# Three layers on one core: the frequency-domain convolution run one half of its frequencies at a time, and an output projection whose first tiles are split in two

## Chip, cores, metric

The kernel runs on one core of one Trainium2 chip. The metric is device time in microseconds (us) of one execution; lower is better.

## What is computed

The reference is a stack of three layers on 512 tokens of 1024 channels, float32. The change lies in the mixer of the first layer, which is two mixers side by side (512 channels each), joined by an output projection:

```python
def _hyena(hy, spec, skip):
    L = hy.shape[1]
    u = hy.astype(jnp.float32)
    z, g1, g2 = u[..., :D_HYENA], u[..., D_HYENA:2 * D_HYENA], u[..., 2 * D_HYENA:]
    for o, gate in enumerate((g1, g2)):
        conv = jnp.fft.irfft(jnp.fft.rfft(z, n=2 * L, axis=1) * spec[:, o], n=2 * L, axis=1)[:, :L]
        z = gate * (conv + z * skip[o].astype(jnp.float32))
    return z

...
        y_hy = _group_rms_norm(_hyena(hy, spec, hy_skip[l]), hy_norm_g[l], HYENA_GROUPS)
...
        y_ml = _group_rms_norm(y_ml, ml_norm_g[l], MLSTM_HEADS)
        mixed = jnp.concatenate([y_hy.astype(h.dtype), y_ml.astype(h.dtype)], axis=-1)
        h = h + mixed @ w_out[l]
```

`spec` is the spectrum of a filter that a small network with sine activations makes from the position, times a decay window. `_group_rms_norm` divides groups of channels by their root mean square. `y_ml` is a gated linear attention; after this layer's mixer come a cross-attention over 256 memory rows, a feed-forward layer, and then a second block of two layers, none of which the change touches.

## The kernel before

Every engine has a program of its own, written out in order; semaphores tie them together. A projection's weights come as panels of 1 MB that SyncE loads into two buffers in turn (`load`, L2556: panel g waits until panel g-2 has been split). ScalarE makes the upper half-precision part of a panel and VectorE the lower one (`split`, L1155 and L1706); TensorE then takes three half-precision products for each pair of tiles (`product`, L366). TensorE writes into two rings of banks of its accumulator memory: ring A with four banks, ring B with three. `reuse` waits until the bank's reader of one turn before has freed it.

The stage that the change touches runs from 259.3 us (the last gate projection `og` ends) to 448.7 us (the sum for the norm of the memory rows begins). Its steps on TensorE, in order, are these:

1. `filters(0)` (L659): eight products make the taps of order 0, four tiles (`tt`) by two directions. VectorE multiplies each with its window and adds and subtracts pairs (`filter_windows`, L2067; `taps`, L2060) into `HS` and `HD`.
2. `head_sums("ml")` (L639) sums the squares of the attention's output, `turn_z(0)` (L670) transposes `z`. ScalarE takes the root (L1200), VectorE its reciprocal (`inverse_rows`, L1798), and `head_roots("ml")` (L647) spreads the result over the partitions. VectorE scales with it (L2098) and makes the lower parts (`low`, L1724); these are input tiles 4 to 7 of the output projection.
3. For each of two orders `o`: `transform("spec")`, the spectrum of the taps, then `transform("zspec")`, the spectrum of z (both L694). Each is cosine and sine (`part`) by even and odd positions (`odd`) by two halves of the frequencies (`kt`), thus eight banks of two products. ScalarE copies each even bank to `EVEN` (L1195); VectorE adds and subtracts the odd bank (`butterfly`, L2117 and L2118), which gives a frequency and its mirror image. Then VectorE takes the complex product: `multiply` (L2126 to L2136), 12 instructions for a half, and `mirror` (L2142, L2143), 4 instructions for a half, which raises the semaphore `mirrored`.
4. The transform back (L711): TensorE waits for `mirrored` of a half and takes that half for all four channel tiles. VectorE adds the skip (L2169), GpSimd multiplies with the gate (L2492), which gives the z of the next order. Between the orders come `filters(1)` and `turn_z(1)`.
5. `head_sums("hy")`, root, reciprocal and `head_roots("hy")` for the convolution's output, input tiles 0 to 3 of the projection (`hy_low`).
6. `project("out", 8, ...)`: tiles 0 and 1 of panel 0 together, over all eight input tiles, then tiles 2 and 3 of panel 1, one after the other. Then `middle` takes the sum for the memory norm (`norm_sum`, L500), which waits for squares that ScalarE makes after it has split three panels (L1434 to L1440), and the last two panels follow in halves of the tokens.

TensorE's and VectorE's loops over one order, as before:

```python
                transform("spec", (HS, HD))
                pe.wait_ge(B.freed_sem(("zt", o, 3)), B.freed_at(("zt", o, 3)))
                transform("zspec", (ZT, ZT))
...
                for kt in range(2):
                    if kt + o:
                        dve.wait_ge(sem("sine_parts"), 4 * o + 2 * kt)
                    for part in range(2):
                        butterfly("zspec", kt, part, ZSP[:, 2 * part, :], ZSP[:, 2 * part + 1, :])
                    when_free(dve, A, ("zspec", o, kt, 1, 1))
                    multiply(2 * kt)
                    if kt:
                        mirror(0)
                    multiply(2 * kt + 1)
                mirror(1)
```

## Time and profile before

| | |
|---|---|
| median of 3 runs | 2122.17 us (2120.74 to 2129.97) |
| the profiled execution | 2120.89 us, span 2119.0 us |
| mean granted clock of TensorE | 0.981 |
| TensorE busy, whole span | 2028.9 us (96%) |
| the stage 259.3 to 448.7 | 189.4 us, TensorE busy 153.09 us |

PE is TensorE, DVE is VectorE, ACT is ScalarE, POOL is GpSimd, SP is SyncE. In the timelines one float32 product of the program is two instructions. A row's time in brackets is how long the engine had stood idle, and the arrow names what released it. In the view by stretches the granted clock is a share of full speed: 1.00 is 2.4 GHz, 0.50 is 1.2 GHz.

### The profile page before, as it was taken

The numbers are of one execution on the slowest core, as the hardware profiler recorded it, in microseconds if no ns is written. First come the engines' busy times: TensorE is split into PE (matmuls) and PEld (weight loads), VectorE is DVE, ScalarE is ACT, GpSimd is POOL, SyncE is SP. The second block draws the span as 40 slices with busy tenths as digits, with TensorE's granted clock in tenths as the row PEclk, the third lists the DMA queues.
The fourth block names the chain that finished last, engine by engine and source line by source line (L and its number), as shares of the span: only waits on it lengthen the run. The fifth ranks groups of instructions, "written<-read, shape, count | busy, mean of one in ns | idle before, by whom it ended". The sixth has DMA issues, their size and how long they took to land.

```text
span 2119.0 us, 27115 instructions
## 1 busy us (share of the span) xinstructions
PE 2028.9 (96%) x11486; PEld 1199.2 (57%) x11486; DVE 946.1 (45%) x1209; ACT 726.8 (34%) x1121; POOL 351.1 (17%) x358
## 2 busy tenths in 40 slices
PE   7999988699999999999999999999999899999997
PEld 5644435366667444488456644446866566444466
DVE  5654565645545333225475422222655645222224
ACT  5432220134434442114363422221454534222213
POOL 1011200011003221003102512110240016121100
PEclk9999988899999999999999999999999999999999
DMA  6211210022222222232222232222221121233321
GB/s 233 80 60 40 77 42 0 0 100 100 100 102 78 100 100 100 100 103 103 75 80 80 76 104 100 100 100 100 80 80 60 40 80 60 99 103 106 111 100 41
DMA packets 28179, 179.65 MB, mean 85 GB/s; under 512 B 2912, under 2 KB 7136, under 8 KB 7136
## 3 DMA queue, kind: packets, MB, share of 16 engines
q1 hardware_dynamic: 27264, 170.93, 23.4%
q10 hardware_dynamic: 512, 4.94, 0.7%
q0 software_dynamic: 288, 2.10, 0.3%
q8 instruction: 91, 1.49, 0.3%
q14 instruction: 24, 0.20, 0.0%
HBM read 175.86 MB, written 2.10 MB: 84 GB/s over the span
## 4 chain that ended last, share of the span: by engine, by line
PE 87%; DVE 9%; ACT 3%; issue 1%; DMA 0%; POOL 0%; ACTq 0%; DVEq 0%
PE psum_a L368 24%; PE psum_a L369 24%; PE psum_a L370 24%; PE psum_b L500 2%; PE psum_a L694 2%; PE psum_a L711 2%; DVE X L1730 1%; PE psum_a L622 1%; PE psum_den L620 1%; DVE RINV L1704 1%; PE psum_a L647 1%; DVE W_PARTS L1710 1%; PE psum_b L600 1%; DVE ARENA L1730 1%; ACT W_PARTS L1160 1%
## 5 line engine op out<-in xcount | busy, mean ns | idle before, releaser
L1710 DVE SCALAR_TENSOR_TENSOR W_PARTS<-W,W_PARTS 128x2048 f16<-128x2048 f32 x145 | 332.6, 2297 | 614.6 <-ACT W_PARTS L1160 614.6
L368 PE MATMUL psum_a<-U,W_PARTS 128*128 128x512 f16 (+1 forms) x1304 | 489.6, 375 | 8.8 <-POOL U L2464 3.9
L369 PE MATMUL psum_a<-U,W_PARTS 128*128 128x512 f16 (+1 forms) x1304 | 489.4, 375 | 0.0
L370 PE MATMUL psum_a<-U,W_PARTS 128*128 128x512 f16 (+1 forms) x1304 | 489.1, 375 | 0.0
L1160 ACT ACTIVATE W_PARTS<-W 128x2048 f16<-128x2048 f32 x145 | 275.7, 1905 | 502.1 <-PE psum_a L370 502.1
L368 PE MATMUL psum_a<-ARENA,W_PARTS 128*128 128x256 f16 (+2 forms) x956 | 295.4, 309 | 3.6 <-DVE W_PARTS L1710 3.0
L369 PE MATMUL psum_a<-ARENA,W_PARTS 128*128 128x256 f16 (+2 forms) x956 | 295.3, 309 | 0.0
L370 PE MATMUL psum_a<-ARENA,W_PARTS 128*128 128x256 f16 (+2 forms) x956 | 295.3, 309 | 0.0
L368 PEld LDWEIGHTS psum_a<-U,W_PARTS 128*128 128x128 f16 x1304 | 128.1, 98 | 158.9 <-DVE W_PARTS L1710 9.6
L370 PEld LDWEIGHTS psum_a<-U,W_PARTS 128*128 128x128 f16 x1304 | 128.1, 98 | 148.2 <-issue 1.6
L369 PEld LDWEIGHTS psum_a<-U,W_PARTS 128*128 128x128 f16 x1304 | 128.1, 98 | 147.4 <-issue 3.8
L2498 POOL TENSOR_TENSOR ARENA<-ARENA 128x512 f16<-128x512 f32 x76 | 118.1, 1574 | 450.4 <-ACT ARENA L1256 450.4
L368 PEld LDWEIGHTS psum_a<-ARENA,W_PARTS 128*128 128x128 f16 (+1 forms) x956 | 93.8, 98 | 49.7 <-DVE W_PARTS L1710 3.3
L368 PE MATMUL psum_a<-MIX,W_PARTS 128*128 128x256 f16 (+1 forms) x384 | 118.8, 309 | 2.1 <-DVE MIX L1724 1.5
L370 PEld LDWEIGHTS psum_a<-ARENA,W_PARTS 128*128 128x128 f16 (+1 forms) x956 | 93.9, 98 | 45.1 <-issue 0.6
L369 PEld LDWEIGHTS psum_a<-ARENA,W_PARTS 128*128 128x128 f16 (+1 forms) x956 | 93.9, 98 | 44.7 <-issue 0.3
L370 PE MATMUL psum_a<-MIX,W_PARTS 128*128 128x256 f16 (+1 forms) x384 | 118.8, 309 | 0.0
L369 PE MATMUL psum_a<-MIX,W_PARTS 128*128 128x256 f16 (+1 forms) x384 | 118.8, 309 | 0.0
L1247 ACT ACTIVATE ARENA<-psum_a 128x512 f32<-128x512 f32 (+1 forms) x84 | 45.7, 552 | 191.8 <-PE psum_a L370 191.7
L2460 POOL TENSOR_TENSOR U<-X,U 128x256 f16<-128x256 f32 x64 | 48.5, 772 | 215.8 <-ACT U L1170 170.5
L1195 ACT ACTIVATE ARENA<-psum_a 128x256 f32<-128x256 f32 (+2 forms) x79 | 35.5, 467 | 128.2 <-PE psum_a L370 83.8
L1889 DVE SCALAR_TENSOR_TENSOR ARENA<-psum_a,ARENA 128x512 f32<-128x512 f32 (+1 forms) x48 | 30.8, 646 | 101.1 <-PE psum_a L370 101.1
(289 smaller groups left out, 2709.2 us busy)
## 6 DMA issues: line engine op xcount, KB each, us to landing
W<-weights SPq DMA_DIRECT2D x159, 1024.0 KB, 4.8
CON<-const ACTq DMA_DIRECT2D x1, 3071.5 KB, 12.2
X<-x_in SPq DMA_DIRECT2D x2, 1024.0 KB, 7.3
U<-dft POOLq DMA_DIRECT2D x1, 1024.0 KB, 5.3
ARENA<-dft POOLq DMA_DIRECT2D x1, 1024.0 KB, 5.2
ARENA<-mem_in ACTq DMA_DIRECT2D x1, 1024.0 KB, 4.7
y_out<-U SPq DMA_DIRECT2D x2, 512.0 KB, 3.0
y_out<-U SPq DMA_DIRECT2D x4, 256.0 KB, 2.2
```

Source lines behind the costliest of these rows:

```text
L368: nc.tensor.matmul(out, left(0), right(0), start=first, stop=False)
L369: nc.tensor.matmul(out, left(0), right(1), start=False, stop=False)
L370: return nc.tensor.matmul(out, left(1), right(0), start=False, stop=last)
L500: last = nc.tensor.matmul(bank[:, 0:HALF], ones, square_tile(kt), start=kt == 0, stop=kt == KT - 1)
L694: last = nc.tensor.matmul(bank[:, :], FDFT[:, part, odd, n, kt * P:(kt + 1) * P], sources[part][:, 2 * odd + n, :], start=n == 0, stop=n == 1)
L711: last = nc.tensor.matmul(banks[ct][:, HALVES[odd]], y[:, 2 * odd + kt, ct * P:(ct + 1) * P], IDFT[:, part, kt, HALVES[odd]], start=kt + p ...
L1160: nc.scalar.activation(HOMES[home_of[g]][:, 0, :], W[g % 2][:, :], ACT.Copy, scale=W_SCALE).then_inc(sem("panel_high"), 1)
L1247: nc.scalar.activation(TS[:, 2 * (j % 2) + m, cols], A.bank(key)[:, 0:cols.stop - cols.start], ACT.Silu if M.gated else ACT.Relu, scale=DE ...
L1710: nc.vector.scalar_tensor_tensor(out=home[:, 1, :], in0=W[g % 2][:, :], scalar=W_SCALE, in1=home[:, 0, :], op0=ALU.mult, op1=ALU.subtract) ...
L1730: nc.vector.scalar_tensor_tensor(out=out(kt, half), in0=src(kt, half), scalar=par(gain, kt), in1=RINV[:, HALVES[half]], op0=ALU.mult, op1= ...
L2460: nc.gpsimd.tensor_tensor(out, src(kt, half), high_part, ALU.subtract).then_inc(sem(f"low_{name}"), 1)
L2498: nc.gpsimd.tensor_tensor(G16[:, 1, n, :], GF[:, n % 4, :], G16[:, 0, n, :], ALU.subtract)\
```

## The change

The same products, copies and element-wise instructions are issued. Their order, some of their buffers and two rings change:

- Each order runs by halves of the frequencies: spectrum of z half 0, of the taps half 0, of z half 1, of the taps half 1. VectorE multiplies and mirrors half 0 before it comes to the taps' half 1. The product tiles of half 0 have buffers of their own (`SQ`, `ROOT`, `RINV`), as `HS` and `HD` are still being read.
- `turn_z(0)` moves ahead of `filters(0)`. `head_roots("ml")` moves behind the first half of z's spectrum; on VectorE the reciprocal, the scaling and the lower parts move with it.
- Three of the eight tap products of order 1 run between the two halves of the transform back of order 0, on ring B. The split of panel 1 of the output projection (`used(("og", 1))`) moves on VectorE from ahead of order 0 to the end of order 0.
- The first four tiles of the output projection each take input tiles 4 to 7 first (`out_tile`): tile 0 ahead of `head_sums("hy")`, tiles 1 and 2 behind it, tile 3 behind `head_roots("hy")`, which now writes to ring B; then each takes input tiles 0 to 3.

```diff
-        YC, YS = HS, HD
+        early = SQ[:, :, :].rearrange("p a b -> p (a b)").rearrange("p (a b) -> p a b", a=2)
+        YC = (early[:, 0, :], HS[:, 1, :], early[:, 1, :], HS[:, 3, :])
+        YS = (ROOT[:, :], HD[:, 1, :], RINV[:, :], HD[:, 3, :])
...
+        def filter_ring(o, tt, d):
+            return B if o and 2 * tt + d < 3 else A
...
-            def filters(o):
-                for tt in range(4):
-                    for d in range(2):
-                        bank = reuse(A, ("filt", o, tt, d))
-                        c = SMALL_W3 + (2 * o + d) * 512
-                        nc.tensor.matmul(bank[:, :], HID[0:64, token_tile(tt)], SMALL[0:64, c:c + 512], start=True, stop=True)\
-                            .then_inc(A.done, 1)
+            def filters(o, numbers):
+                for n in numbers:
+                    tt, d = divmod(n, 2)
+                    R = filter_ring(o, tt, d)
+                    bank = reuse(R, ("filt", o, tt, d))
+                    c = SMALL_W3 + (2 * o + d) * 512
+                    nc.tensor.matmul(bank[:, :], HID[0:64, token_tile(tt)], SMALL[0:64, c:c + 512], start=True, stop=True)\
+                        .then_inc(R.done, 1)
...
+            turn_z(0)
             pe.wait_ge(sem("sine"), 2)
-            filters(0)
+            filters(0, range(8))
             head_sums("ml", 4, lambda h: EVEN[:, h, :], one_row)
-            turn_z(0)
-            head_roots("ml", 4, ROWS[0:64, 3, :], row_back)
+            pe.wait_ge(sem("fdft_landed"), 16)
             for o in range(2):
-                if o:
-                    filters(1)
-                    turn_z(1)
+                pe.wait_ge(B.freed_sem(("zt", o, 3)), B.freed_at(("zt", o, 3)))
+                transform("zspec", o, 0, (ZT, ZT))
                 if o == 0:
-                    pe.wait_ge(sem("fdft_landed"), 16)
+                    head_roots("ml", 4, ROWS[0:64, 3, :], row_back)
                 pe.wait_ge(sem("taps"), 8 * (o + 1))
-                def transform(what, sources):
-                    for kt in range(2):
-                        for part in range(2):
-                            for odd in range(2):
-                                bank = reuse(A, (what, o, kt, part, odd))
-                                for n in range(2):
-                                    last = nc.tensor.matmul(bank[:, :], FDFT[:, part, odd, n, kt * P:(kt + 1) * P],
-                                                            sources[part][:, 2 * odd + n, :], start=n == 0, stop=n == 1)
-                                last.then_inc(A.done, 1)
-                transform("spec", (HS, HD))
-                pe.wait_ge(B.freed_sem(("zt", o, 3)), B.freed_at(("zt", o, 3)))
-                transform("zspec", (ZT, ZT))
+                transform("spec", o, 0, (HS, HD))
+                transform("zspec", o, 1, (ZT, ZT))
+                transform("spec", o, 1, (HS, HD))
                 if o == 0:
                     pe.wait_ge(sem("idft_landed"), 16)
-                banks = [reuse(A, ("y", o, ct)) for ct in range(4)]
-                for kt in range(2):
-                    pe.wait_ge(sem("mirrored"), 2 * o + kt + 1)
-                    for ct in range(4):
-                        for odd in range(2):
-                            for part, y in ((0, HC), (1, HSN)):
-                                last = nc.tensor.matmul(banks[ct][:, HALVES[odd]], y[:, 2 * odd + kt, ct * P:(ct + 1) * P],
-                                                        IDFT[:, part, kt, HALVES[odd]], start=kt + part + odd == 0, stop=kt + part + odd == 3)
-                        if kt == 1:
-                            last.then_inc(A.done, 1)
+                inverse_transform(o, 0)
+                if o == 0:
+                    filters(1, range(3))
+                inverse_transform(o, 1)
+                if o == 0:
+                    filters(1, range(3, 8))
+                    turn_z(1)
...
+            def out_tile(j, tiles):
+                if len(out_panels) <= j // 2:
+                    w, g = panel()
+                    panel_of.setdefault("out", g)
+                    out_panels.append((w.rearrange("p l (k c) -> p l k c", k=KT), g))
+                w, g = out_panels[j // 2]
+                bank = A.bank(("out", j)) if ("out", j) in A.at else reuse(A, ("out", j))
+                for kt in tiles:
+                    pe.wait_ge(sem("hy_low" if kt < 4 else "ml_low"), kt % 4 + 1)
+                    last = product(bank[:, :], lambda l: w[:, l, kt, (j % 2) * P:(j % 2 + 1) * P], lambda l: MIX16[:, l, kt, :],
+                                   kt == 4, kt == 3)
+                    if kt == 3:
+                        last.then_inc(A.done, 1)
+                        released[g] = A.done, A.at["out", j] + 1
+            out_tile(0, range(4, 8))
             head_sums("hy", 4, lambda h: PR[h], lambda ct: half[:, 62 - 2 * ct:126 - 2 * ct])
-            head_roots("hy", 4, ZT[0:64, 0, :], lambda ct: gback[:, ct, :])
-            project("out", 8, MIX16, first_wait=lambda kt: pe.wait_ge(sem("hy_low" if kt < 4 else "ml_low"), kt % 4 + 1),
-                    tail="x", middle=lambda: norm_sum("mem", 0))
+            out_tile(1, range(4, 8))
+            out_tile(2, range(4, 8))
+            head_roots("hy", 4, ZT[0:64, 0, :], lambda ct: gback[:, ct, :], B)
+            out_tile(3, range(4, 8))
+            for j in range(4):
+                out_tile(j, range(4))
+            tile_list["out"] = [(("out", j), j, slice(0, T), j // 2 if j % 2 else None) for j in range(4)]
+            project("out", 8, MIX16, tail="x", middle=lambda: norm_sum("mem", 0), first=2)
...
+            def turned(o):
+                for tt in range(4):
+                    copy_out(B, ("zt", o, tt), ZT[:, tt, :], B.bank(("zt", o, tt))[:, :])
+            def even_copies(what, o, kt):
+                for part in range(2):
+                    if what == "spec":
+                        when_free(act, A, ("zspec", o, kt, part, 1))
+                    elif o:
+                        when_free(act, A, ("spec", 0, kt, part, 1))
+                    key = (what, o, kt, part, 0)
+                    copy_out(A, key, EVEN[:, 2 * kt + part, :], A.bank(key)[:, :])
+            turned(0)
...
-            used(("og", 1))
-            for tt in range(4):
-                copy_out(B, ("zt", 0, tt), ZT[:, tt, :], B.bank(("zt", 0, tt))[:, :])
-            for h in range(4):
-                key = ("rn", "ml", h)
-                high(A.freed_sem(key), A.freed_at(key), MIX16[:, 0, 4 + h, :], QK[:, h, :], "ml_high")
             for o in range(2):
-                for tt in range(4 * o):
-                    copy_out(B, ("zt", o, tt), ZT[:, tt, :], B.bank(("zt", o, tt))[:, :])
-                for what in ("spec", "zspec"):
-                    for kt in range(2):
-                        for part in range(2):
-                            n = 2 * kt + part
-                            if what == "zspec":
-                                when_free(act, A, ("spec", o, kt, part, 1))
-                            elif o:
-                                when_free(act, A, ("zspec", 0, kt, part, 1))
-                            key = (what, o, kt, part, 0)
-                            copy_out(A, key, EVEN[:, n, :], A.bank(key)[:, :])
+                even_copies("zspec", o, 0)
+                if o == 0:
+                    for h in range(4):
+                        key = ("rn", "ml", h)
+                        high(A.freed_sem(key), A.freed_at(key), MIX16[:, 0, 4 + h, :], QK[:, h, :], "ml_high")
+                even_copies("spec", o, 0)
+                even_copies("zspec", o, 1)
+                even_copies("spec", o, 1)
+                if o == 0:
+                    used(("og", 1))
+                    turned(1)
             for ct in range(4):
                 act.wait_ge(sem("z_gated"), 5 + ct)
...
-                high(A.freed_sem(key), A.freed_at(key), MIX16[:, 0, ct, :], HY[:, ct, :], "hy_high")
+                high(B.freed_sem(key), B.freed_at(key), MIX16[:, 0, ct, :], HY[:, ct, :], "hy_high")
...
-            filter_windows(0)
-            inverse_rows("ml", ROWS[0:64, 3, :], ROWS[0:64, 2, :])
...
-                low("ml_high", h + 1, MIX16[:, 1, 4 + h, :], QK[:, h, :], MIX16[:, 0, 4 + h, :], "ml_low")
-            used(("og", 1))
-            for o in range(2):
-                if o:
-                    filter_windows(1)
...
-                def multiply(n):
-                    kt, sign = n // 2, n % 2
+            def multiply(o, kt):
+                when_free(dve, A, ("spec", o, kt, 1, 1))
...
...
+            dve.wait_ge(sem("ml_gated"), 4)
+            for o in range(2):
+                butterflies("zspec", o, 0)
+                if o == 0:
+                    inverse_rows("ml", ROWS[0:64, 3, :], ROWS[0:64, 2, :])
+                    ml_norm()
+                    dve.wait_ge(sem("ml_low"), 4)
                 dve.wait_ge(sem("taps"), 8 * (o + 1))
+                butterflies("spec", o, 0)
+                multiply(o, 0)
+                dve.wait_ge(sem("sine_parts"), 4 * o + 2)
+                butterflies("zspec", o, 1)
+                mirror(o, 0)
+                butterflies("spec", o, 1)
+                multiply(o, 1)
+                mirror(o, 1)
                 if o == 0:
-                    dve.wait_ge(sem("ml_low"), 4)
-                for kt in range(2):
-                    for part, h in ((0, HC), (1, HSN)):
-                        butterfly("spec", kt, part, h[:, kt, :], h[:, 2 + kt, :])
-                for kt in range(2):
-                    if kt + o:
-                        dve.wait_ge(sem("sine_parts"), 4 * o + 2 * kt)
-                    for part in range(2):
-                        butterfly("zspec", kt, part, ZSP[:, 2 * part, :], ZSP[:, 2 * part + 1, :])
-                    when_free(dve, A, ("zspec", o, kt, 1, 1))
-                    multiply(2 * kt)
-                    if kt:
-                        mirror(0)
-                    multiply(2 * kt + 1)
-                mirror(1)
+                    filter_windows(1, range(3))
...
+                if o == 0:
+                    dve.wait_ge(sem("mirrored"), 2)
+                    filter_windows(1, range(3, 8))
+                    used(("og", 1))
             inverse_rows("hy", ZT[0:64, 0, :], ZT[0:64, 1, :])
             for ct in range(4):
-                scale_rows(("rn", "hy", ct), HY[:, ct, :], HY[:, ct, :], par("hy_norm", ct))
+                scale_rows(("rn", "hy", ct), HY[:, ct, :], HY[:, ct, :], par("hy_norm", ct), B)
```

## Rows read from the trace of the kernel before

**Rows 1.** The page: TensorE in 40 slices of the span; the chain that ended last.

```profile
PE   7999988699999999999999999999999899999997
...
PE 87%; DVE 9%; ACT 3%; issue 1%; DMA 0%; POOL 0%; ACTq 0%; DVEq 0%
```

**Rows 2.** Stretches: length; busy of PE, PEld, DVE, ACT, POOL; clock; DMA; GB/s.

```profile
259.30:448.70 189.40, 153.09 (x449) 78.96 (x449) 112.41 (x162) 34.56 (x52) 12.77 (x11) 0.88 0.08 28
274.70:284.90 10.20, 10.20 (x12) 3.85 (x13) 5.36 (x9) 2.52 (x4) 0.00 (x0) 0.50 0.00 0
321.50:325.80 4.30, 4.24 (x10) 3.47 (x11) 4.26 (x8) 0.00 (x0) 0.00 (x0) 0.50 0.00 0
349.70:353.10 3.40, 3.35 (x4) 1.51 (x5) 0.00 (x0) 0.00 (x0) 0.00 (x0) 0.51 0.00 0
389.70:394.10 4.40, 4.37 (x10) 3.53 (x11) 4.37 (x8) 0.00 (x0) 0.00 (x0) 0.50 0.00 0
414.00:424.80 10.80, 9.24 (x15) 3.18 (x16) 5.40 (x8) 2.52 (x4) 0.00 (x0) 0.53 0.00 0
1080.00:1110.00 30.00, 25.86 (x194) 17.90 (x192) 23.25 (x42) 18.45 (x40) 0.00 (x0) 1.00 0.25 89
```

**Rows 3.** Timeline of TensorE: start, duration, instructions; in brackets idle before, and releaser.

```profile
266.33 3.65 PE L639 MATMUL psum_b<-U,CON 128*64 128x512 f32 x8
...
273.04 0.74 PE L670 MATMUL psum_b<-CON,ARENA 128*128 128x128 f32 x4 [1.42 <-ACT ARENA L1195]
274.60 7.14 PE L647 MATMUL psum_a<-ARENA,CON 64*128 64x512 f32 x8 [0.82 <-DVE ARENA L1798]
...
321.56 16.18 PE L711 MATMUL psum_a<-ARENA 128*128 128x256 f32 x64 [10.55 <-DVE ARENA L2143]
337.67 7.14 PE L659 MATMUL psum_a<-SMALL,MU 64*128 64x512 f32 x16
344.74 2.18 PE L670 MATMUL psum_b<-CON,ARENA 128*128 128x128 f32 x16
349.75 29.42 PE L694 MATMUL psum_a<-ARENA,U 128*128 128x512 f32 x64 [2.83 <-DVE ARENA L2065]
...
414.03 6.63 PE L647 MATMUL psum_a<-ARENA,CON 64*128 64x512 f32 x8 [4.15 <-DVE ARENA L1798]
422.20 0.58 PE L368 MATMUL psum_a<-MIX,W_PARTS 128*128 128x512 f16 x1 [1.53 <-DVE MIX L1724]
...
448.73 3.65 PE L500 MATMUL psum_b<-SQ,CON 128*128 128x256 f32 x8 [4.35 <-ACT SQ L1143]
...
1100.92 2.61 PE L732 MATMUL psum_b<-CON,MIX 128*128 128x128 f32 x20 [1.66 <-ACT ARENA L1223]
```

**Rows 4.** Timeline of VectorE in the stage.

```profile
271.21 3.34 DVE L1798 RECIPROCAL ARENA<-ARENA 64x512 f32<-64x512 f32 x1
...
305.56 0.69 DVE L2126 TENSOR_TENSOR MIX<-ARENA 128x512 f32<-128x512 f32 x1
...
312.80 0.68 DVE L2117 TENSOR_TENSOR ARENA<-U,psum_a 128x512 f32<-128x512 f32 x1
...
406.00 0.75 DVE L2169 SCALAR_TENSOR_TENSOR ARENA<-ARENA,PAR,psum_a 128x512 f32<-128x512 f32 x1 [0.98 <-PE psum_a L711]
...
436.06 2.29 DVE L1710 SCALAR_TENSOR_TENSOR W_PARTS<-W,W_PARTS 128x2048 f16<-128x2048 f32 x1 [1.31 <-ACT W_PARTS L1160]
```

**Rows 5.** Timeline of ScalarE in the stage.

```profile
408.12 0.63 ACT L1426 ACTIVATE MIX<-ARENA 128x512 f32<-128x512 f32 x1 [1.09 <-POOL ARENA L2492]
409.91 0.68 ACT L1200 ACTIVATE ARENA<-psum_b,EPS 64x512 f32<-64x512 f32 x1 [1.16 <-PE psum_b L639]
...
434.12 1.91 ACT L1160 ACTIVATE W_PARTS<-W 128x2048 f16<-128x2048 f32 x1 [12.00 <-PE psum_a L370]
```

**Rows 6.** Timeline of GpSimd at the end of the stage.

```profile
406.83 1.26 POOL L2492 TENSOR_TENSOR ARENA<-ARENA 128x512 f32<-128x512 f32 x1 [0.46 <-DVE ARENA L2169]
```

**Rows 7.** The page: DMA issues, size of each and time to landing.

```profile
W<-weights SPq DMA_DIRECT2D x159, 1024.0 KB, 4.8
```

More of the change, by code:

```diff
@@ L671, in turn_z, with transform @@
                     last.then_inc(B.done, 1)
+            def transform(what, o, kt, sources):
+                for part in range(2):
+                    for odd in range(2):
+                        bank = reuse(A, (what, o, kt, part, odd))
+                        for n in range(2):
+                            last = nc.tensor.matmul(bank[:, :], FDFT[:, part, odd, n, kt * P:(kt + 1) * P],
+                                                    sources[part][:, 2 * odd + n, :], start=n == 0, stop=n == 1)
+                        last.then_inc(A.done, 1)
@@ new lines, in inverse_transform @@
+            def inverse_transform(o, kt):
+                pe.wait_ge(sem("mirrored"), 2 * o + kt + 1)
+                for ct in range(4):
+                    bank = A.bank(("y", o, ct)) if kt else reuse(A, ("y", o, ct))
+                    for odd in range(2):
+                        for part, y in ((0, HC), (1, HSN)):
+                            last = nc.tensor.matmul(bank[:, HALVES[odd]], y[:, 2 * odd + kt, ct * P:(ct + 1) * P],
+                                                    IDFT[:, part, kt, HALVES[odd]], start=kt + part + odd == 0, stop=kt + part + odd == 3)
+                    if kt:
+                        last.then_inc(A.done, 1)
@@ L2162, in _, with mirror @@
-                mirror(1)
+                    nc.vector.tensor_tensor(YS[tile], PR[2], PR[3], ALU.add).then_inc(sem("product"), 1)
+            def mirror(o, kt):
+                dve.wait_ge(sem("product"), 8 * o + 4 * kt + 4)
+                for y, h in ((YC, HC), (YS, HSN)):
+                    nc.vector.tensor_tensor(h[:, kt, :], y[kt], y[2 + kt], ALU.add)
+                    last = nc.vector.tensor_tensor(h[:, 2 + kt, :], y[kt], y[2 + kt], ALU.subtract)
+                last.then_inc(sem("mirrored"), 1)
```

77 lines of the change are left out of this document (43 added, 34 removed).

## Prediction, made before the changed kernel ran

> **What bounds the kernel now.** I read the page first. In the slices of the span [rows 1] the reader is to see that TensorE is at nine tenths or more almost everywhere, except in the sixth to ninth of the slices of 53 us and the last one; the chain that ended last is 87% TensorE and 9% VectorE. So elsewhere only less work on TensorE would help, while this stage has something to win without any. Then the view by stretches [rows 2]: from 259.3 to 448.7 us the stage takes 189.4 us, of which TensorE is busy 153.1, so it stands idle 36.3. Five stretches show a clock of 0.50 while it works: busy 10.2, 4.2, 3.4, 4.4 and 9.2 us at half speed, whose halves are lost: 5.1 + 2.1 + 1.7 + 2.2 + 4.6 = 15.7 us. Work at full speed in the stage is thus 153.1 - 15.7 = 137.4 us, and 52.0 us are idleness and its aftermath.
>
> TensorE's timeline [rows 3] says where the idle time lies: 1.4 + 0.8 ahead of head_roots("ml"), 10.6 ahead of the transform back in each of the two orders (the row of order 0 stands), 2.8 between the orders, 4.2 ahead of head_roots("hy"), 1.5 ahead of the output projection, 4.4 ahead of the memory norm's sum. VectorE's timeline [rows 4] shows the cause of the large ones: from the first product (305.56) to the next butterfly (312.80) are 12 instructions in 7.24 us, so 0.60 us apiece, and TensorE has nothing of its own to do until half 0 is mirrored.
>
> **Prices.** A bank of the forward transform: (29.42 - 1.7 lost to the clock) / 16 banks = 1.73 us, so four banks, one half of one spectrum, 6.9. A half of the transform back: (16.18 - 2.1) / 2 = 7.0. A tap product 7.14 / 8 = 0.9; turn_z 2.2; head_sums 3.65 [rows 3]. Half of the input tiles for one output tile: from 422.20 to 448.73 - 4.35 = 444.38 are 22.2 us, less 1.3 for the low clock at its start (to 424.8 [rows 2]), over 8 half tiles: 2.6. On VectorE: a butterfly is 2 instructions, 1.2; the products of a half 7.2; a mirror 4 instructions and a wait, 2.5; a reciprocal 3.3 [rows 4]. A hand-over between engines is 0.05 to 0.2: from the start of the root (409.91) to head_roots (414.03) are 4.12 us for 0.68 + 3.34 of work [rows 3 to 5].
>
> **The change, gap by gap.** The instructions are the same, so 137.4 us stay. I work out each gap that the new order leaves.
>
> The beginning. turn_z(0) and filters(0) take 9.3 us, head_sums 3.65, then comes z's half 0 with nothing to wait for: ScalarE's four copies and four squares, each about as long as the 0.63 of such a square [rows 5], fit under turn and filters. The gaps of 1.4 and 0.8 go. (a) Behind z's half 0 stands head_roots("ml"), which waits for the reciprocal, and that is now queued on VectorE behind both butterflies of z. After the last bank: 0.2 + 1.2 + 3.3 + 0.1 = 4.7 us idle. This is the new wait that the change adds; everything in TensorE's queue stands behind it.
>
> (b) In order 0 the taps' half 1 needs a bank that the first butterfly of z's half 1 frees. VectorE comes to it after the last bank of the taps' half 0 by 0.2 + 1.2 + 7.2 + 1.2 + 0.1 = 9.9; TensorE has z's half 1 and one more bank, 6.9 + 1.7 = 8.6. Gap 1.3. (c) The transform back of half 1 waits for the second mirror: after the last bank of the taps' half 1, 0.2 + 1.2 + 7.2 + 2.5 + 0.1 = 11.2; TensorE has the transform back of half 0 and three tap products, 7.0 + 2.7 = 9.7. Gap 1.5. Half 0 itself is mirrored 1.2 + 2.5 after the butterfly of (b), while TensorE still has three banks, 5.2, to do: no gap. (d) Between the orders, five tap products (4.5) and turn_z (2.2) cover gating and windows; the last copy of z's transposes remains, 0.7. (e) Order 1 as (b), 1.3. (f) Order 1 as (c), but without tap products: 11.2 - 7.0 = 4.2.
>
> The end. The last channel tile passes skip 0.75, gate 1.26 and square 0.63 [rows 4 to 6], 2.9 with the hand-overs; out_tile(0) with 2.6 and the first of the four head sums lie in front. Root and reciprocal, 4.1 to 4.3, lie behind out_tile(1) and (2), 5.2; scaling and the first lower part, the gap of 1.5 of before [rows 3], behind out_tile(3), 2.6. No gap, and the 4.2 and 1.5 go.
>
> (g) The memory norm's sum. Before, three splits stood in front of it, two of them behind the last output tile: 4.4. The two first panels now end only two half tiles apart, not two whole ones. Panel 19 may be loaded once panel 17 is split. Counted from the end of tile 1: ScalarE 1.91 [rows 5], VectorE 2.29 [rows 4], the load 4.8 [rows 7], its split by ScalarE with a first square 2.4 (the old gap of 4.35 less one split of 1.91), hand-overs 0.4: 11.8. TensorE has tiles 2 and 3, 5.2. Gap 6.6, so 2.2 more than before. This load was hidden; it is late now.
>
> Sum of the gaps: 4.7 + 1.3 + 1.5 + 0.7 + 1.3 + 4.2 + 6.6 = 20.3, against 36.3: 16.0 us less.
>
> **The clock.** After (a) head_roots stands in the same place as before, where from 274.7 to 284.9 the clock was 0.50 [rows 2]: I take the same 5.1. The gap (f) is like the 4.4 ahead of 448.73 or the 2.8 ahead of 349.75; the latter was followed by 3.4 us at 0.50, price 1.7, and the gaps of 10.6 cost 2.1 and 2.2: I take 2.0, with ends 0 and 4.6 (the last stretch of before). The gaps of 0.7 to 1.5 I cost at nothing, as in 1080 to 1110 there is one of 1.66 and the clock stayed 1.00 [rows 2, 3]; the other bound is the pair 1.4 and 0.8, after which it did fall. The output projection starts warm. So 7.1 lost against 15.7: 8.6 less. Here a page speaks against the change. The Trainium skill ("TensorE: Matmul & The Clock Gate", section "HAM oscillation — how this bites in real kernels") says that work cut up by waits pays for the drop of the clock again at every wait, rather than once. By that rule the change, which makes one gap of 10.6 into several, would win 5 to 7 us less and come out at 2101 to 2103, against 2096.3 by the rows; the row at 1100.92 does not bear it out for short gaps.
>
> **Moved work with cover.** Panel 1's split (VectorE 2.3, from about 285 to 341 us) delays only the first butterfly of order 1, by about 1 us, and the next bank comes later than that. On SP's queue the load of panel 18 moves with it, to about 343; ScalarE wants it near 414, so 65 us cover 4.8. GpSimd's load of the inverse tables waits for the attention's lower parts, about 294 instead of 285, and is wanted near 313. Without these covers each would cost its 2 to 5 us. The new product buffers are of the same shape in the same memory: nothing.
>
> **Sum.** 16.0 + 8.6 = 24.6 us less. The profiled execution took 2120.9 us (1.9 more than its span), so 2096.3. The median of the runs shown is 1.3 above that execution, the lowest 0.15 below; I stay with the execution's base. Behind 448.7 nothing changes, it only comes earlier.
>
> **The rivals.**
>
> - *The clock recovers sooner.* After (a) only one short stretch (1.7 instead of 5.1) and none after (f): 5.4 less, 2091 (3.4 + 2.0). For it: 3.4 us at 353.1 was all that followed a gap of 2.8. Against: head_roots ran wholly at 0.50 twice [rows 2, 3]. Chance 0.17; without any low clock 2089.
> - *Every small gap costs the clock too, or a bank comes one step later.* (b), (c) and (e) each followed by a low stretch of 1.7 to 2.2: 5 to 7 more, 2101 to 2103. A bank freed one butterfly later in (b) and (e) gives 2.4, 2099. For it: the pair 1.4 and 0.8. Against: the row at 1100.92. Chance 0.24.
> - *The waits only change names.* The work VectorE does per order, not its order, is the limit, or the load of (g) meets other traffic, and the gaps stay near 30 us: win under 10, 2111 and more. Against: in the stage VectorE is busy 112 of 189 us [rows 2]. Chance 0.06.
> - *Slower: the clock stays low after (a) through order 0.* There lie three spectrum halves, the transform back, taps and turn: 20.8 + 14.0 + 7.1 + 2.2 = 44 us of full-speed work, so 44 more, less 1.6 counted and about 3.5 of gaps that it fills: 39 more, 2135. It decides for slower once the low clock lasts some 49 us longer than counted, as each us of it loses half. Against: at 284.9, 3.2 us into the spectrum, it was back [rows 2, 3]. Chance 0.03.
>
> **How the numbers follow.** My forecast, 2093 to 2099, has 0.50; the rivals have 0.17, 0.24, 0.06 and 0.03. The range 2088 to 2105 takes in the first three cases with the bounds of the clock (2089 and 2103) and 1 to 2 us for the base; it leaves out about 0.1 to 0.15. A measurement of this kernel tells 0.5%, 10.6 us, from no change: faster by more needs less than about 2111, which is the forecast and the first two rivals with most of what lies between, 0.92; within it 0.05; slower 0.03.
>
> **What would show it.** The changed profile should show no gap over 5 us on TensorE between 259 and the end of the four output tiles, a gap of 4 to 5 ahead of L647's "ml" rows with the reciprocal as releaser, one near 4 ahead of the last transform back, 1 to 1.5 at the odd banks of the taps' half 1, none ahead of the output's half-precision products, and the memory norm's sum starting near 424 after some 6.6 idle. The prediction is wrong if head_roots is not preceded by such a gap, if the clock is 0.50 for much more than 14 us of busy time before that sum, or if the stage after it no longer lies as before.

## The result, and the profile after

| | median us | lowest to highest, runs | ratio to before, 95% interval |
|---|---|---|---|
| before | 2122.88 | 2120.74 to 2129.97, 4 | |
| after | 2102.26 | 2099.62 to 2107.32, 4 | 0.9905, 0.9891 to 0.992 |

The change makes the kernel 20.6 us faster, 0.95%. The forecast was 2096.3 with a range of 2088 to 2105: the time lies in the range and 6 us above the forecast, outside the 2093 to 2099 that was given half of the chance. The profiled execution of the changed kernel took 2102.12 us with a span of 2100.2, against 2120.9 with 2119.0, so the span shrank by 18.8 us where 24.6 were forecast.

The page of the changed kernel, in TensorE's slices and the chain that ended last, answers to [rows 1]. The sixth to ninth slices read 8, 9, 9, 8 where those of before read 8, 8, 6, 9; the chain is 87% TensorE and 9% VectorE, as before.

```profile
PE   7999989989999999999999999999999899999997
```

TensorE's timeline of the changed stage answers to [rows 3]: start, duration, instructions, and in brackets the idle time before and its releaser. In this kernel's lines L654 is head_roots, L687 the forward transform, L698 the transform back, L1839 the reciprocal, L2160 a butterfly, L2187 the mirror, L1231 a copy, L507 the norm's sum and L1179 the squares.

```profile
260.02 2.08 PE L678 MATMUL psum_b<-CON,ARENA 128*128 128x128 f32 x16
...
272.68 7.13 PE L687 MATMUL psum_a<-ARENA,U 128*128 128x512 f32 x16
284.51 7.19 PE L654 MATMUL psum_a<-ARENA,CON 64*128 64x512 f32 x8 [4.70 <-DVE ARENA L1839]
291.63 18.33 PE L687 MATMUL psum_a<-ARENA,U 128*128 128x512 f32 x36
311.37 5.42 PE L687 MATMUL psum_a<-ARENA,U 128*128 128x512 f32 x12 [1.41 <-DVE ARENA L2160]
...
328.12 8.61 PE L698 MATMUL psum_a<-ARENA 128*128 128x256 f32 x32 [1.65 <-DVE ARENA L2187]
...
344.05 22.58 PE L687 MATMUL psum_a<-ARENA,U 128*128 128x512 f32 x52 [0.72 <-ACT ARENA L1231]
368.04 5.42 PE L687 MATMUL psum_a<-ARENA,U 128*128 128x512 f32 x12 [1.41 <-DVE ARENA L2160]
...
384.79 8.86 PE L698 MATMUL psum_a<-ARENA 128*128 128x256 f32 x32 [4.42 <-DVE ARENA L2187]
...
405.04 3.70 PE L654 MATMUL psum_b<-ARENA,CON 64*128 64x512 f32 x8
...
428.61 3.75 PE L507 MATMUL psum_b<-SQ,CON 128*128 128x256 f32 x8 [6.82 <-ACT SQ L1179]
432.16 2.54 PE L507 MATMUL psum_b<-ARENA,CON 128*128 128x256 f32 x8
```

The gaps are 4.70, 1.41, 1.65, 0.72, 1.41, 4.42 and 6.82 us: the seven that were forecast, each at its place and behind the releaser named for it, 21.1 us in sum against 36.3 before. None of 10.6 is left. The "hy" rows of head_roots (405.04) have nothing in brackets, and take 3.70 us where the "ml" rows (284.51) take 7.19 behind their gap; that pair is the price of the low clock on eight instructions of one shape.

The view by stretches answers to [rows 2]; its columns are the same (length; busy of PE, PEld, DVE, ACT, POOL; clock; DMA share; GB/s).

```profile
259.90:428.60 168.70, 147.58 (x450) 76.32 (x449) 112.60 (x162) 34.73 (x52) 12.75 (x11) 0.93 0.10 33
284.50:297.20 12.70, 12.69 (x15) 4.86 (x16) 5.40 (x8) 3.11 (x5) 0.59 (x1) 0.51 0.08 13
327.90:331.40 3.50, 3.27 (x9) 2.69 (x10) 1.97 (x4) 0.00 (x0) 0.00 (x0) 0.55 0.00 0
385.90:389.40 3.50, 3.50 (x11) 2.83 (x10) 0.75 (x1) 0.00 (x0) 0.78 (x1) 0.55 0.00 0
428.60:433.80 5.20, 5.19 (x13) 4.15 (x14) 1.79 (x1) 2.01 (x7) 0.00 (x0) 0.53 0.82 290
```

The stage takes 168.7 us instead of 189.4, with VectorE busy 112.6 us in it, as before (112.4). The other rows are the stretches at low clock: behind the reciprocal (clock 0.51), behind the mirror of order 0 (0.55), behind that of order 1 (0.55), and in the memory norm's sum (0.53). What they cost is read from durations of the same work at 1.00: behind the reciprocal 7.19 + 18.33 against 3.70 + 15.72 (the last pair stands in a kernel below), 6.1 us; then 8.61 and 8.86 against 7.17 for the transform back of a half, 1.4 and 1.7; and in the norm's sum 3.75 + 2.54 against 1.97 + 1.89, 2.4.

Why the gap of 4.70 is there is to be seen on VectorE. The rows are its timeline ahead of head_roots: the first instruction of the last butterfly of z's first half (0.69 us, the second is like it), then the reciprocal of 3.34 us that stands behind it in the queue.

```profile
279.92 0.69 DVE L2159 TENSOR_TENSOR ARENA<-U,psum_a 128x512 f32<-128x512 f32 x1 [2.12 <-PE psum_a L687]
...
281.12 3.34 DVE L1839 RECIPROCAL ARENA<-ARENA 64x512 f32<-64x512 f32 x1
```

TensorE was done with z's half at 279.8 (272.68 + 7.13). The root that the reciprocal needs had been ready since 273.47, as ScalarE's row shows, and VectorE stood idle ahead of 279.92 for a bank:

```profile
272.79 0.68 ACT L1236 ACTIVATE ARENA<-psum_b,EPS 64x512 f32<-64x512 f32 x1 [6.42 <-PE psum_b L646]
```

And ScalarE's timeline ahead of the norm's sum: the split of panel 18, then that of panel 19, which waited for its load, and behind it the squares. Ahead of them stands SyncE's row, which issues that load.

```profile
421.11 0.33 SPq L2612 DMA_DIRECT2D W<-weights  x1
...
421.89 1.91 ACT L1196 ACTIVATE W_PARTS<-W 128x2048 f16<-128x2048 f32 x1 [3.27 <-PE psum_a L376]
426.16 1.91 ACT L1196 ACTIVATE ARENA<-W 128x2048 f16<-128x2048 f32 x1 [2.36 <-DMA W<-weights]
...
428.07 1.32 ACT L1179 ACTIVATE SQ<-ARENA 128x256 f32<-128x256 f32 x4
```

From the issue at 421.11 to the split at 426.16 are 5.0 us. The load itself is thus about as long as the 4.8 us of the median load [rows 7]; it is late because of when it was issued.

### The profile page after: what moved, and what is told of

Same layout as the page of the kernel before. It is cut to its first block, busy times and chain, and to the rows that moved or that the text cites. A ratio compares the mean times of both kernels' runs of the same rounds, so it can differ in the third digit from the quotient of the medians.

```text
span 2100.2 us, 27114 instructions
## 1 busy us (share of the span) xinstructions
PE 2025.5 (96%) x11486; PEld 1197.9 (57%) x11486; DVE 946.0 (45%) x1209; ACT 727.0 (35%) x1121; POOL 351.2 (17%) x358
## 4 chain that ended last, share of the span: by engine, by line
PE 87%; DVE 9%; ACT 3%; issue 1%; DMA 1%; POOL 0%; ACTq 0%; DVEq 0%; SPq 0%
PE psum_a L374 24%; PE psum_a L375 24%; PE psum_a L376 24%; PE psum_b L507 2%; PE psum_a L687 2%; DVE X L1771 1%; PE psum_a L629 1%; PE psum_den L627 1%; DVE RINV L1745 1%; DVE W_PARTS L1751 1%; PE psum_a L698 1%; ACT W_PARTS L1196 1%; PE psum_b L607 1%; DVE ARENA L1771 1%; PE psum_b L1021 1%
## 5 line engine op out<-in xcount | busy, mean ns | idle before, releaser
L1231 ACT ACTIVATE ARENA<-psum_a 128x256 f32<-128x256 f32 (+2 forms) x79 | 35.5, 467 | 128.5 <-PE psum_a L376 84.1
```

The costliest lines, as they stand in the source:

```text
L1231: nc.scalar.activation(out, src, func, scale=scale).then_inc(R.freed_sem(key), 1)
```

## The experiments

The kernels ran in two groups, the first four and the last four of the table, each group beside the kernel before on the same chip. Before had a median of 2122.57 us (2120.42 to 2123.61, 8 runs) in the first group and 2122.43 (2120.81 to 2129.91, 7 runs) in the second.

| kernel | median us | lowest to highest | ratio to before, 95% interval |
|---|---|---|---|
| after_again | 2100.16 | 2099.88 to 2102.86 | 0.990, 0.9884 to 0.9917 |
| conv_only | 2113.85 | 2110.56 to 2116.70 | 0.9955, 0.9939 to 0.9972 |
| out_only | 2113.80 | 2113.49 to 2115.61 | 0.9961, 0.9947 to 0.9976 |
| recip_first | 2091.16 | 2090.62 to 2092.16 | 0.9854, 0.9838 to 0.9871 |
| warm_a | 2094.90 | 2094.15 to 2100.60 | 0.9873, 0.9847 to 0.9899 |
| warm_all | 2089.93 | 2088.43 to 2096.67 | 0.9852, 0.9825 to 0.9879 |
| squares_first | 2095.53 | 2093.30 to 2097.80 | 0.9867, 0.9844 to 0.9891 |
| best | 2082.44 | 2081.29 to 2082.63 | 0.9805, 0.9784 to 0.9827 |

The theory going in: gaps as the forecast names them, made by VectorE's queue and by the late load of panel 19, and on top a price for the clock behind the longer ones. Its rivals: the gaps are only a symptom of VectorE's total work, and the work behind them is slow for a reason of its own.

### after_again: the changed kernel once more

No edit. It is the base for the kernels below and a second look at the clock.

> The changed kernel once more, beside the three below. Both theories: ratio to before 0.989 to 0.992. Of the clock: if the low stretches behind the short gaps are a matter of chance of each execution, the profile shows gaps of the same lengths (4.7, 1.4, 1.7, 0.7, 1.4, 4.4, 6.8 us) but another set of low stretches than in the first profile.

It took 2100.16 us. TensorE's timeline, where it differs from the rows above:

```profile
292.32 16.90 PE L687 MATMUL psum_a<-ARENA,U 128*128 128x512 f32 x36
...
327.36 7.17 PE L698 MATMUL psum_a<-ARENA 128*128 128x256 f32 x32 [1.63 <-DVE ARENA L2187]
...
426.02 3.75 PE L507 MATMUL psum_b<-SQ,CON 128*128 128x256 f32 x8 [6.44 <-ACT SQ L1179]
429.56 2.74 PE L507 MATMUL psum_b<-ARENA,CON 128*128 128x256 f32 x8
```

The gaps are the same to a few hundredths, but for the last, 6.44 instead of 6.82 (there the load of panel 19 took 4.7 us, from 418.90 to 423.57, instead of 5.0). The clock is not the same. Behind the 4.70 the spectrum's 36 products take 16.90 us instead of 18.33. Behind the mirror of order 0, where the gap is 1.63 instead of 1.65, the transform back takes 7.17 instead of 8.61: no low clock. So the same kernel differs by 2.9 us between two executions in its clock alone, with nothing in its order of work that differs. The stretch of the low clock behind the reciprocal, 12.7 us in the changed kernel's first profile, is 10.2 here:

```profile
284.90:295.10 10.20, 9.90 (x12) 3.87 (x13) 5.16 (x9) 2.52 (x4) 0.00 (x0) 0.52 0.01 2
```

### conv_only: the convolution by halves without the split output projection

Against the changed kernel:

```diff
-            out_tile(0, range(4, 8))
...
-            head_roots("hy", 4, ZT[0:64, 0, :], lambda ct: gback[:, ct, :], B)
-            out_tile(3, range(4, 8))
...
-            project("out", 8, MIX16, tail="x", middle=lambda: norm_sum("mem", 0), first=2)
+            head_roots("hy", 4, ZT[0:64, 0, :], lambda ct: gback[:, ct, :])
+            project("out", 8, MIX16, first_wait=lambda kt: pe.wait_ge(sem("hy_low" if kt < 4 else "ml_low"), kt % 4 + 1),
+                    tail="x", middle=lambda: norm_sum("mem", 0))
```

> The convolution by halves alone; the output projection, and head_roots of the convolution on ring A, as before the change. Theory (the gain is the sum of gaps and their low clock): the gaps 4.2 and 1.5 ahead of head_roots and of the output projection come back with about 3 us of low clock, the memory norm's gap goes back from 6.8 to 4.4: 13 to 14 us faster than before, ratio 0.994. Rival (the halves bring nothing by themselves, VectorE being the limit): within 4 us of before.

It took 2113.85 us, 8.7 less than before where 13 to 14 were expected. TensorE's timeline shows the gaps of the first half of the stage as in the changed kernel, and at its end the three of before, 4.15, 1.53 and 4.35, with the low clock at all of them:

```profile
399.97 7.19 PE L654 MATMUL psum_a<-ARENA,CON 64*128 64x512 f32 x8 [4.15 <-DVE ARENA L1816]
408.69 0.58 PE L374 MATMUL psum_a<-MIX,W_PARTS 128*128 128x512 f16 x1 [1.53 <-DVE MIX L1742]
...
435.20 3.65 PE L507 MATMUL psum_b<-SQ,CON 128*128 128x256 f32 x8 [4.35 <-ACT SQ L1156]
438.69 1.89 PE L507 MATMUL psum_b<-ARENA,CON 128*128 128x256 f32 x8
```

The norm's sum begins at 435.20, 13.5 us earlier than the 448.73 of before: in the stage the expectation holds. But this execution's span, 2114.8, is only 4.2 shorter. The rest was lost behind the stage, in work that no edit touches, and most of it in one piece of the next odd layer. The view by stretches, of conv_only and then of the kernel before:

```profile
1620.00:1760.00 140.00, 129.26 (x763) 88.43 (x762) 79.36 (x141) 63.62 (x122) 20.67 (x26) 0.91 0.13 46
...
1633.50:1773.50 140.00, 129.80 (x824) 90.42 (x824) 85.16 (x147) 69.43 (x130) 27.66 (x32) 0.96 0.13 46
```

The clock is 0.91 against 0.96, so some 0.05 of 140 us, 7 us, were lost. Two pieces of work ahead of and behind the loss say the same, TensorE's rows of conv_only first and those of the kernel before second:

```profile
1597.83 4.63 PE L1017 MATMUL psum_a<-MIX,ARENA 128*128 128x128 f32 x40
...
1690.40 3.81 PE L1072 MATMUL psum_a<-ARENA 128*128 128x128 f32 x32 [0.94 <-ACT ARENA L1242]
```

```profile
1610.43 4.63 PE L1004 MATMUL psum_a<-MIX,ARENA 128*128 128x128 f32 x40
...
1696.28 3.81 PE L1059 MATMUL psum_a<-ARENA 128*128 128x128 f32 x32 [0.94 <-ACT ARENA L1229]
```

The first piece comes 12.6 us earlier than before, the second only 5.9. So 6.7 of the 9.3 us that were lost behind the stage (13.5 - 4.2) lie between the two. The four runs of conv_only fall in two pairs, 2116.70 and 2116.53 at a mean clock of 0.980, and 2111.17 and 2110.56 at 0.982; only one of the first pair was profiled. That the pairs differ by this stretch is likely and not shown. The faster pair is 11.7 us below before and comes near what was expected.

### out_only: the split output projection with the old convolution

Against the kernel before:

```diff
-            head_roots("hy", 4, ZT[0:64, 0, :], lambda ct: gback[:, ct, :])
-            project("out", 8, MIX16, first_wait=lambda kt: pe.wait_ge(sem("hy_low" if kt < 4 else "ml_low"), kt % 4 + 1),
-                    tail="x", middle=lambda: norm_sum("mem", 0))
+            out_tile(0, range(4, 8))
...
+            head_roots("hy", 4, ZT[0:64, 0, :], lambda ct: gback[:, ct, :], B)
+            out_tile(3, range(4, 8))
...
+            project("out", 8, MIX16, tail="x", middle=lambda: norm_sum("mem", 0), first=2)
```

> The split output projection alone, the convolution as before the change. Theory: gaps of 4.2 and 1.5 and the low clock of 4.6 us go, the memory norm's gap grows by 2.4: 7 to 8 us faster than before, ratio 0.9965. Rival (the load behind the earlier last tiles takes it all back): within 2 us of before.

It took 2113.80 us, 8.8 less than before. The two gaps of 10.55 stand, and the end of the stage is that of the changed kernel:

```profile
321.60 16.26 PE L712 MATMUL psum_a<-ARENA 128*128 128x256 f32 x64 [10.55 <-DVE ARENA L2167]
...
417.51 3.70 PE L648 MATMUL psum_b<-ARENA,CON 64*128 64x512 f32 x8
...
440.77 3.75 PE L501 MATMUL psum_b<-SQ,CON 128*128 128x256 f32 x8 [6.51 <-ACT SQ L1167]
```

head_roots("hy") has no gap and takes 3.70 us; the norm's sum waits 6.51, against the 4.35 of before and of conv_only. So the output part of the change alone makes the new wait of 2.2 us, and wins in spite of it: 3.6 us of gaps (36.3 to 32.7) and the low clock of head_roots and the first products behind it. The two parts alone win 8.7 + 8.8 = 17.5 us, together 22.4 (after_again); with the faster pair of conv_only, 11.7 + 8.8 = 20.5. The parts add up to within what the clock moves.

### recip_first: the reciprocal ahead of z's butterflies

```diff
+                if o == 0:
+                    inverse_rows("ml", ROWS[0:64, 3, :], ROWS[0:64, 2, :])
                 butterflies("zspec", o, 0)
                 if o == 0:
-                    inverse_rows("ml", ROWS[0:64, 3, :], ROWS[0:64, 2, :])
                     ml_norm()
```

> The changed kernel with VectorE's reciprocal of the attention's norm ahead of the two butterflies of z's half 0 instead of behind them. Theory: TensorE's gap of 4.7 us ahead of head_roots goes, as the reciprocal ends while z's half 0 still runs, and with it the 6.2 us of low clock behind it: 9 to 11 us faster than the changed kernel. Rival (the clock falls behind head_sums and in head_roots whether or not there is a gap, as it did before the change): 4.7 us faster only, the clock 0.50 through head_roots.

It took 2091.16 us, 9.0 less than after_again: within what the theory said of the queue and the clock, and far from the 4.7 of the gap alone. The timeline:

```profile
279.44 3.70 PE L654 MATMUL psum_a<-ARENA,CON 64*128 64x512 f32 x8
283.07 15.72 PE L687 MATMUL psum_a<-ARENA,U 128*128 128x512 f32 x36
...
316.93 8.78 PE L698 MATMUL psum_a<-ARENA 128*128 128x256 f32 x32 [1.64 <-DVE ARENA L2187]
```

No gap ahead of head_roots, 3.70 us instead of 7.19, and the spectrum 15.72 instead of 16.90 or 18.33. One wait cost 4.7 us of idleness and 4.7 to 6.1 of low clock behind it. Behind the mirror of order 0 the gap of 1.64 was followed by the low clock here (8.78 instead of 7.17).

### warm_a and warm_all: the gaps stay, TensorE is kept at work in them

Both add products of constants into a bank that nothing reads. They are no part of the reference and only fill the waits. In warm_a five stand ahead of head_roots("ml"); warm_all has those, one ahead of the second transform back of order 0, five ahead of that of order 1, and seven ahead of the memory norm's sum.

```diff
+                    for n in range(5):
+                        nc.tensor.matmul(psum_den[:, :], ones, ones_wide, start=True, stop=True)
```

> The changed kernel with five idle products (ones by ones, 128x512, float32, some 4.3 us, into a bank that nobody reads) ahead of head_roots of the attention. They do none of the reference's work; head_roots waits for the reciprocal as long as before. Theory (half of the loss behind this gap is the low clock): the reciprocal comes at the same time, but head_roots takes 3.7 instead of 7.2 us and the spectrum behind it runs at 1.00: 5 to 6 us faster than the changed kernel. Rival (head_roots on 64 rows is slow or throttled of itself): no change, 0 to 1 us.

> As warm_a, with idle products also ahead of the second half of the transform back (one in order 0, five in order 1) and seven ahead of the memory norm's sum, so that TensorE hardly stands still in the stage. Theory (the 3.7 us by which the prediction missed are low clock behind the gaps): all low stretches between 259 and 440 us go; 9 to 11 us faster than the changed kernel, 2090 to 2092. Rival (the clock falls by other things than idleness, short gaps included): under 7 us faster, low stretches remain.

warm_a took 2094.90 us, 5.3 less than after_again. Its timeline has head_roots at 284.24, where the changed kernel has it (284.51), at 3.70 us:

```profile
284.24 3.70 PE L654 MATMUL psum_a<-ARENA,CON 64*128 64x512 f32 x8 [0.41 <-DVE ARENA L1841]
287.87 15.72 PE L687 MATMUL psum_a<-ARENA,U 128*128 128x512 f32 x36
```

This separates wait and aftermath. The wait is as long as before, but what follows it runs at full speed, and the time falls by what the low clock cost. That head_roots is slow by itself is refuted.

warm_all took 2089.93 us, 10.2 less than after_again. The rows behind three of the four filled waits:

```profile
322.02 7.17 PE L698 MATMUL psum_a<-ARENA 128*128 128x256 f32 x32 [0.59 <-DVE ARENA L2193]
...
377.25 7.17 PE L698 MATMUL psum_a<-ARENA 128*128 128x256 f32 x32
...
419.01 1.97 PE L507 MATMUL psum_b<-SQ,CON 128*128 128x256 f32 x8 [0.43 <-ACT SQ L1185]
```

The transform back takes 7.17 us both times and the norm's sum 1.97. From after_again's durations the low clock behind its gaps costs 9.0 us (4.7 + 0 + 1.7 + 2.6), and these are gone. The 10.2 measured hold something else as well, which lies outside the stage. About 50 us behind the norm's sum every kernel has a wait of 3.02 us that no edit touches; after_again has the low clock behind it and warm_all has not, which is worth about 1.7 us (0.47 of the first row's 3.60). The view by stretches, of after_again and of warm_all:

```profile
478.90:482.50 3.60, 3.58 (x18) 2.58 (x19) 2.82 (x3) 0.00 (x0) 0.00 (x0) 0.53 0.67 223
...
469.30:472.90 3.60, 3.58 (x33) 3.22 (x34) 3.16 (x4) 0.38 (x1) 0.00 (x0) 1.00 0.65 216
```

So 9.0 us is the price of the clock behind the gaps of after_again, of which 6.4 lie in the stage, where 7.1 were forecast, and 2.6 in the norm's sum, where none were.

### squares_first: the memory's squares ahead of panel 19's split

```diff
-            split(panel_of["out"] + 4)
             squares("mem", 0, in_mem)
+            split(panel_of["out"] + 4)
```

> The changed kernel with ScalarE's squares of the memory rows ahead of its split of weight panel 19 instead of behind it. Theory (the memory norm's gap of 6.8 us waits for the load of panel 19 and for that split, which the sum doesn't need): the gap falls to about 2.5, which is one split and one square; 4 us faster than the changed kernel, and 1 to 2 more where the clock holds. Rival (the split is needed soon after, so the wait moves to the memory's key projection): no change.

It took 2095.53 us, 4.6 less than after_again. ScalarE's timeline, where the squares now follow the split of panel 18 at 422.61, and TensorE's at that place:

```profile
424.52 1.32 ACT L1179 ACTIVATE SQ<-ARENA 128x256 f32<-128x256 f32 x4
```

```profile
425.06 1.97 PE L507 MATMUL psum_b<-SQ,CON 128*128 128x256 f32 x8 [2.55 <-ACT SQ L1179]
```

The squares no longer wait for a load that they don't need. The gap is 2.55 us instead of 6.44 to 6.82, and the sum is not slowed: 1.97 us instead of 3.75. So the wait was indeed that for the load of panel 19, through ScalarE's queue. The gap and the norm's sum give 3.9 + 2.6 = 6.5 us against after_again, more than the 4.6 of the medians: in this profile the low clock behind (a) and behind the mirror of order 0 cost 3.1 us more than in after_again (7.19 + 18.51 and 8.70 against 7.19 + 16.90 and 7.17).

### best: the two orders together, and a half output tile in the last long gap

It takes recip_first and squares_first, and puts the half of output tile 0 that is ready early between the two halves of the transform back in order 1, into a bank of its own (psum_den, ring E). The other output tiles move up by one.

```diff
+        E = Ring([psum_den], sem("e_done"), [sem("e_free")])
...
+                if o == 1:
+                    out_tile(0, range(4, 8))
                 inverse_transform(o, 1)
...
-            out_tile(0, range(4, 8))
+            out_tile(1, range(4, 8))
...
```

> The changed kernel with three edits: the reciprocal first, the squares first, and the first output tile's half moved between the two halves of the transform back of order 1, into a bank of its own. Theory: 9 from the reciprocal, 4 from the squares, 2.6 less idle ahead of the transform back but 1.5 ahead of the first tile over the convolution's input, so 1 to 3 from the third: 14 to 17 us faster than the changed kernel, about 2085. Rival (the edits share their gain, as each only keeps the clock up): 9 to 10, about 2091.

It took 2082.44 us, 17.7 less than after_again and 40.0 less than before; its interval, 0.9784 to 0.9827, lies wholly below the 0.9884 to 0.9917 of after_again. That is just above the 14 to 17 expected. TensorE's timeline:

```profile
280.13 3.70 PE L655 MATMUL psum_a<-ARENA,CON 64*128 64x512 f32 x8
...
317.63 8.86 PE L699 MATMUL psum_a<-ARENA 128*128 128x256 f32 x32 [1.65 <-DVE ARENA L2191]
...
374.55 7.17 PE L699 MATMUL psum_a<-ARENA 128*128 128x256 f32 x32 [1.83 <-DVE ARENA L2191]
...
398.25 0.39 PE L375 MATMUL psum_den<-MIX,W_PARTS 128*128 128x512 f16 x1 [1.45 <-DVE MIX L1768]
...
411.33 1.97 PE L508 MATMUL psum_b<-SQ,CON 128*128 128x256 f32 x8 [2.55 <-ACT SQ L1182]
```

The gap of 4.42 has become 1.83 (2.6 us of products fill it) and is no longer followed by the low clock, 7.17 us for the transform back. A gap of 1.45 ahead of the output's lower parts is new, since less work stands ahead of them. With 1.41, 0.72 and 1.41 as in the changed kernel the gaps sum to 11.0 us against 21.1, and one low stretch is left between 260 and 415 us, behind the 1.65. By the rows the third edit is worth 2.6 + 1.7 (8.86 to 7.17) - 1.45 = 2.8 us, within the 1 to 3 expected of it. The squares bring 6.5 and not the 4 counted, the reciprocal 4.7 + 4.7 less the 1.7 of low clock behind the 1.65: 17.0 in sum.

## Why the prediction was right

**The gaps.** This is where the forecast stood on firm ground. Forecast and measured, in the order (a) to (g): 4.7 and 4.70; 1.3 and 1.41; 1.5 and 1.65; 0.7 and 0.72; 1.3 and 1.41; 4.2 and 4.42; 6.6 and 6.82. In sum 20.3 and 21.1. Each is off by a tenth or two; the forecast's own terms for (a) add up to 4.8 and not to the 4.7 written. These small errors were not taken apart. That (a) is VectorE's queue was shown by recip_first; that (g) is the wait for the load of panel 19, by squares_first; that it comes with the output part alone and is 2.2 more than before, by out_only (6.51 against 4.35). For (b) to (f) the releaser in the rows is the one that the forecast names; no experiment moved VectorE's work there.

**The clock.** This is the term that was mis-sized. Forecast were 5.1 behind (a), 2.0 behind (f) and nothing behind the rest: 7.1 us. In the profiled execution it was 6.1, 1.7 and 1.4 behind (c): 9.2. The forecast took (a) from before, where head_roots stood behind 1.4 + 0.8 us of idleness; here the low clock lasted longer in this execution, and in after_again the price was 4.7. The step "the gaps of 0.7 to 1.5 I cost at nothing" held for (b), (d) and (e) in every kernel, and for (c) in after_again, conv_only and warm_a; it failed for (c) in after, recip_first, squares_first and best. Of the signs named for a wrong prediction, that of more than 14 us of busy time at half speed ahead of the norm's sum fell on both sides: about 18 us in the first profile, twice the 9.2, and 13 in after_again. The clock of before was read a little too high as well: in 414.0 to 424.8 the row's clock is 0.53, so 10.2 of the 10.8 us were low and 1.5 of those idle, which makes 4.3 us lost and not the 4.6 of 9.2 halved.

**What lies outside the stage.** The forecast said that behind 448.7 nothing changes. The norm's sum, right behind (g), took 6.3 us against 5.5 behind the old gap (3.65 + 1.89, as in conv_only), 0.8 more; the forecast gave the longer wait its length and no price in clock. And the stage began at 260.02 instead of 259.3. As its beginning lies between 259.25 (conv_only) and 260.70 (after_again) with the same work ahead of it, those 0.7 us are no effect of the change.

**The ledger.** The norm's sum was forecast near 424 and began at 428.61; of the 24.6 us forecast, 18.8 came in the end. Missing are 0.8 in the gaps, 2.1 in the clock of the stage, 0.8 in the norm's sum, 0.7 ahead of the stage; 1.0 in the stage (189.4 - 168.7 = 20.7 us saved, which is 1.0 short of 24.6 - 0.8 - 2.1) and 0.4 behind it. Of the 1.0 in the stage 0.3 is the misread clock of before. Most of the rest can be seen in the rows as work that takes a little longer in more pieces: at full clock the spectra of order 0 take 7.13 + 15.72 (recip_first) + 5.42 = 28.3 us where the forecast had 27.7, the two halves of a transform back 7.07 + 7.17 = 14.2 where it had 14.0. The forecast held this work to be unchanged. The 0.4 stays open.

**The same sum for after_again.** In after_again the stage took 165.3 us (260.70 to 426.02), where the forecast had 164.8, as its clock lost 6.4 us and not 9.2. So the forecast of the clock was short by 2.1 us in one execution and 0.7 too high in another of the same kernel; which of them was profiled first is chance. The medians, 2102.26 and 2100.16, lie in the range and above the 2099 at which the forecast's own case ends, and one single run, 2107.32, lies above the range.

**The rivals.** The time, 2102, is the number that the second rival gave, but not wholly for its reason: one of its three small gaps was followed by the low clock, and that cost 1.4 us of the 6. The rule of the Trainium skill that the forecast weighed ("TensorE: Matmul & The Clock Gate", section "HAM oscillation — how this bites in real kernels"), that work cut by waits pays for the clock at every wait, held behind the unfilled gaps of 4.1 us and more in each profile, behind 1.65 in some, and in the eight profiles of kernels with the new order never behind a 1.41 or 0.72 that stood alone; in the kernel before the pair of 1.42 and 0.82 was followed by it. The first rival, an early recovery, did not happen in any unaided kernel: behind (a) the price was 4.7 us or more. The waits did more than change names, as 15.2 us of them went. And the clock came back behind (a) after some 10 to 13 us, so the slower rival had its mechanism and not its length.

## What to carry to other kernels

When an order is rearranged, write the gaps out one by one from the queue of the engine that releases each, and give every gap of several microseconds a second price for the clock behind it: here one wait of 4.7 us cost 9.0, and most of what was left to win lay in two instructions that stood behind others that they didn't need. Ask of each instruction that an engine waits in whether the one behind it needs that wait; moving the reciprocal and the squares ahead won 9.0 and 4.6 us with the same instructions. A part of the kernel that no edit touches can still move the time by several microseconds through the clock, so compare positions in the stage as well as whole times.

## What the runs showed that was not expected

The granted clock is not a function of the order of work alone. With the same gap (1.63 and 1.65 us) ahead of the same transform back, the clock stayed at 1.00 in after_again and fell to 0.50 in after: 7.17 and 8.61 us. Behind the same 4.70 us it was low over about 10 us in one and 12.7 in the other. In conv_only an untouched stretch of 140 us had a clock of 0.91 against 0.96 before. Behind 1.83 and 2.55 us in best it stayed at 1.00, while 2.83 us in the kernel before were followed by 0.51 [rows 2, 3]. What decides whether it falls is left open.
